# Summing modulation rows over partitions: on VectorE by 32x32 blocks, with one TensorE batch per phase

## The reference

```
def modulate(x, w, shift, scale):
    return rmsnorm(x, w) * (1 + scale) + shift

def modulation(cond, w_mod, b_mod):
    m = jax.nn.silu(cond) @ w_mod + b_mod
    return jnp.split(m, N_MOD, axis=-1)
...
        sh1, sc1, g1, sh2, sc2, g2, sh3, sc3, g3 = modulation(c[:, None, :], w_mod[l], b_mod[l])
        ch1, cs1, cg1, ch2, cs2, cg2, ch3, cs3, cg3 = modulation(c_ctx[None, None, :], w_mod[l], b_mod[l])
...
        x = x + 0.5 * g1 * swiglu(modulate(x, nw[0], sh1, sc1), ffn1_up[l], ffn1_down[l])
```

## Time and profile before

| | |
|---|---|
| median of three executions | 3129.01 us |
| profiled execution, whole | 3129.19 us |
| its span in the trace | 3127.4 us |
| mean granted TensorE clock | 0.99 |
| TensorE products busy | 3052.9 us, 98% |
| VectorE busy | 1511.2 us, 48% |
| ScalarE busy | 810.9 us, 26% |
| GpSimd busy | 213.0 us, 7% |
| read from HBM | 269.77 MB, mean 87 GB/s |

### The profile page before, as it was taken

The page is one execution under the profiler, slowest core; times in us unless marked ns, Lnnn a source line. Parts: engine busy times, 40 slices in busy tenths (PEclk is TensorE's granted clock), DMA queues, the critical chain, the costliest instruction groups (busy, mean ns, idle before and its releaser), DMA issues.

```text
span 3127.4 us, 43300 instructions
## 1 busy us (share of the span) xinstructions
PE 3052.9 (98%) x16692; PEld 2597.6 (83%) x16692; DVE 1511.2 (48%) x2649; ACT 810.9 (26%) x1094; POOL 213.0 (7%) x212
## 2 busy tenths in 40 slices
PE   7999999999999999999999999999999899999998
PEld 3888888888888888888888888888888778878886
DVE  2555565557533346656655652222236654443333
ACT  2221111233332232212112311121224333332223
POOL 1000000011600010000000100000010510100001
PEclk8999999999999999999999999999999999999999
DMA  6344343221112224344342332222112113333331
GB/s 207 95 127 115 109 129 112 76 69 48 28 41 63 72 61 131 103 128 121 113 127 79 95 104 61 61 60 67 57 46 68 48 51 97 98 87 94 94 93 63
DMA packets 455603, 273.42 MB, mean 87 GB/s; under 512 B 9754, under 2 KB 453828, under 8 KB 455492
## 3 DMA queue, kind: packets, MB, share of 16 engines
q1 hardware_dynamic: 453348, 267.90, 29.9%
q10 hardware_dynamic: 2144, 4.00, 0.4%
HBM read 269.77 MB, written 2.10 MB: 87 GB/s over the span
## 4 chain that ended last, share of the span: by engine, by line
PE 91%; DVE 5%; ACT 2%; issue 1%; DMA 0%; POOL 0%; ACTq 0%; DVEq 0%; POOLq 0%
PE ps L1221 53%; PE ps L1228 27%; PE ps L1371 2%; PE ps L1292 2%; PE ps L1252 1%; PE ps L1376 1%; PE ps L1331 1%; DVE hlo L1716 1%; DVE states L1033 1%; DVE htmp L1706 1%; PE ps L673 1%; PE ps L1270 1%; PE ps L642 1%; PE ps L653 1%; PE ps L557 0%
## 5 line engine op out<-in xcount | busy, mean ns | idle before, releaser
L1221 PE MATMUL ps<-hhi,whi 128*128 128x512 f32 x3136 | 901.0, 355 | 0.0
L1221 PE MATMUL ps<-hlo,whi 128*128 128x512 f32 x3136 | 887.1, 350 | 0.0
L1635 DVE TENSOR_TENSOR wlo<-wraw,whi 128x1024 fp32r<-128x1024 f32 x371 | 456.8, 1232 | 654.7 <-ACT whi L1465 651.0
L1465 ACT ACTIVATE whi<-wraw 128x1024 fp32r<-128x1024 f32 x371 | 391.5, 1056 | 1019.8 <-PE ps L1228 988.3
L1228 PE MATMUL ps<-hhi,wlo 128*128 128x512 f32 x3136 | 633.5, 351 | 0.0
L1221 PEld LDWEIGHTS ps<-hhi,whi 128*128 128x128 f32 x3136 | 503.2, 189 | 84.3 <-issue 3.1
L1221 PEld LDWEIGHTS ps<-hlo,whi 128*128 128x128 f32 x3136 | 502.4, 189 | 85.1 <-issue 0.5
L1228 PEld LDWEIGHTS ps<-hhi,wlo 128*128 128x128 f32 x3136 | 500.5, 188 | 84.7 <-issue 1.0
L1650 DVE SCALAR_TENSOR_TENSOR macc<-modraw,cond,macc 128x256 f32<-128x256 f32 x896 | 365.5, 479 | 0.0
L1221 PE MATMUL ps<-mhi,whi 128*128 128x512 f32 (+1 forms) x1184 | 335.8, 351 | 2.6 <-DVE mlo L1848 1.5
L1221 PE MATMUL ps<-mlo,whi 128*128 128x512 f32 (+1 forms) x1184 | 334.3, 349 | 0.0
(11 more groups left out here) (180 smaller groups left out, 2373.2 us busy)
## 6 DMA issues: line engine op xcount, KB each, us to landing
wraw<-in_ffn_up SPq DMA_DIRECT2D x176, 512.0 KB, 3.9
modraw<-in_w_mod SPq DMA_DIRECT2D x66, 1024.0 KB, 5.2
wraw<-in_ffn_down SPq DMA_DIRECT2D x64, 512.0 KB, 3.7
wraw<-in_w_in SPq DMA_DIRECT2D x64, 512.0 KB, 4.0
wraw<-in_ffn_down SPq DMA_DIRECT2D x32, 384.0 KB, 3.1
wraw<-in_w_out SPq DMA_DIRECT2D x16, 512.0 KB, 3.6
first_mod<-in_w_mod SPq DMA_DIRECT2D x6, 1024.0 KB, 12.0
wraw<-in_w_br_pool SPq DMA_DIRECT2D x16, 256.0 KB, 2.7
```

Of the source, the lines that this page charges most:

```text
L1221: nc.tensor.matmul(o, whi[:, slot, k, :], a[:, k * NT + t0:k * NT + t0 + n], start=(k == 0 and a is hi), stop=False)
L1465: nc.scalar.activation(whi[:, slot2], wraw[:, slot4], ACT.Copy).then_inc(hi_split, 1)
L1635: nc.vector.tensor_tensor(wlo[:, slot2], wraw[:, slot4], whi[:, slot2].bitcast(F32), ALU.subtract).then_inc(lo_split, 1)
```

## The change

It has three parts.

In the loop, VectorE does the sum over partitions nearly by itself. `mod_reduce` turns `macc` (128 x 512) in blocks of 32 x 32, so that what stood on 32 partitions stands in 32 neighbouring columns, and adds these. Four groups of 32 partitions are left, 16 columns for a job (`mred`). TensorE adds the four groups once per phase instead of once per job: `mod_sums` is four products with `fold`, a 128 x 32 matrix of four stacked identities. They run behind the first unit of the next phase, and `mod_finish` follows in VectorE's first pair of that phase, for all jobs of the phase before; gates made from them move behind it. The first pair of such a phase is taken out of the loop.

At the start, VectorE makes jobs 0 to 3 in two groups (`first_accumulate`), and one-column products sum them (`first_sums`); TensorE makes jobs 4 to 7 in the old way. The transfers go in the order 0, 1, 4, 5, 2, 3, 6, 7.

ScalarE takes the norm's root ahead of its first two weight splits, and the semaphore of the constants is cut in two, so that TensorE's first instruction waits for the identity and not for the mask.

```
+FIRST_ORDER = (0, 1, 4, 5, 2, 3, 6, 7)
...
+    fold = sb("fold", [P, BLK])
...
+    def jobs_pending(ph):
+        before = plan[plan.index(ph) - 1] if ph is not plan[0] else ph
+        return before if before["jobs"] and ph is not plan[0] else None
...
-            def mod_sums(job, buf):
-                pe.wait_ge(mod_step, DC * 2 * (job + 1 - START_JOBS))
-                for c in range(2):
-                    for h in range(2):
-                        mm = nc.tensor.matmul(bank(6, 2 * c + h, 1), macc[:, buf, c, h * P:(h + 1) * P],
-                                              ones[:, 0:1], start=True, stop=True)
+            def mod_sums(ph):
+                n0, n1 = jobs_of(ph)
+                pe.wait_ge(mod_reduced, n1 - START_JOBS)
+                at = plan.index(ph) % 2, n0 - ph["job"], n1 - ph["job"]
+                for q in range(P // BLK):
+                    mm = nc.tensor.matmul(bank(6, 0, 4 * (n1 - n0))[BLK * q:BLK * (q + 1)], fold[:],
+                                          mred[:, at[0], at[1]:at[2], q:JOB_COLS:P // BLK], start=True, stop=True)
                 mm.then_inc(mod_sum, 1)
...
-            pe.wait_ge(s_const, 32)
+            pe.wait_ge(s_ident, 16)
...
-            pe.wait_ge(cond_ready, 1)
-            both = cond[:].rearrange("p (c k) -> p k c", c=2)
-            for j in range(START_JOBS):
-                if j == START_JOBS // 2:
-                    norm_sum(BOTH, SQ_ADDED, DC)
-                    pe.wait_ge(rec_ready, 1)
...
+            first_products(VEC_JOBS)
+            first_products(VEC_JOBS + 1)
+            norm_sum(BOTH, SQ_ADDED, DC)
+            first_sums(0)
+            pe.wait_ge(rec_ready, 1)
+            for b in range(NBLK):
+                mm = nc.tensor.transpose(bank(6, b * P, P), tok[:, b:b + 1].to_broadcast([P, P]), ident[:])
+            mm.then_inc(bc_ready, 1)
+            first_products(VEC_JOBS + 2)
+            transpose_first_mod(0)
+            first_products(VEC_JOBS + 3)
+            first_sums(1)
+            transpose_first_mod(1)
...
-                            if jobs:
-                                mod_sums(j0 + 2 * i + h, (j0 + h) % 2)
+                                if first and isinstance(i, int) and i == 0 and jobs_pending(ph):
+                                    mod_sums(jobs_pending(ph))
...
+            act.wait_ge(set_up, 1)
+            root(0, BOTH)
             split_hi(0, 0, 0)
-            act.wait_ge(set_up, 1)
             split_hi(*second_unit(plan[0]))
-            root(0, BOTH)
...
+            def mod_reduce(ph, job, buf, i, h):
+                dve.wait_ge(mod_step, DC * 2 * (job + 1 - START_JOBS))
+                nc.vector.transpose(htmp[:, 0, 0:4 * P], macc[:, buf].rearrange("p c n -> p (c n)")).then_inc(mod_turned, 1)
+                dve.wait_ge(mod_turned, job + 1 - START_JOBS)
+                at = JOB_COLS * (8 * (plan.index(ph) % 2) + h)
+                nc.vector.tensor_reduce(mred[:].rearrange("p a j n -> p (a j n)")[:, ds(2 * JOB_COLS * i + at, JOB_COLS)],
+                                        htmp[:, 0, 0:4 * P].rearrange("p (j n) -> p j n", n=BLK),
+                                        mybir.AxisListType.X, ALU.add).then_inc(mod_reduced, 1)
...
+            def first_accumulate(i):
+                for j in (2 * i, 2 * i + 1):
+                    dve.wait_ge(first_loaded[j], 16)
+                columns = first_mod[:, 2 * i:2 * i + 2]
+                for k in range(DC):
+                    if i == 1 and k == DC // 2:
+                        reciprocals(0, BOTH)
+                    for c in range(2):
+                        acc = first_acc[:, 2 * i:2 * i + 2, c, :]
+                        scalar = cond[:, c * DC + k:c * DC + k + 1]
+                        if k == 0:
+                            ins = nc.vector.tensor_scalar(acc, columns[:, :, 0, :], scalar, None, ALU.mult)
+                        else:
+                            dve.wait_ge(first_step, 2 * DC * i + 2 * k - 1 + c)
+                            ins = nc.vector.scalar_tensor_tensor(out=acc, in0=columns[:, :, k, :], scalar=scalar, in1=acc,
+                                                                 op0=ALU.mult, op1=ALU.add)
+                        ins.then_inc(first_step, 1)
...
+                            if h == 0 and isinstance(i, int) and i == 0 and jobs_pending(ph):
+                                mod_finish(jobs_pending(ph))
+                                if needs_gates:
+                                    make_gates()
                             if jobs:
                                 mod_accumulate(job, (j0 + h) % 2, range(DC // 2, DC))
+                                mod_reduce(ph, job, (j0 + h) % 2, i, h)
```

More of the change, by code:

```diff
@@ L60 @@
 SQ_ADDED = DC - 2
-FIRST_BANKS = (4, 0, 1, 2)
+FIRST_BANKS = (4, 0)
+VEC_JOBS = 4
+BLK = 32
+JOB_COLS = 2 * 2 * P // BLK
+FIRST_ORDER = (0, 1, 4, 5, 2, 3, 6, 7)
 POOL_REC = GRID_H + GRID_W
@@ L248, in build @@
     mrow = lay("mrow", [P, 4 * P])
[L249 removed]
+    mod_row = lay("mod_row", [P, 2 * P * (START_JOBS - VEC_JOBS)])
+    lay.done()
+    lay = Layout()
+    lay.skip(111, "pad_first")
+    first_acc = lay("first_acc", [P, VEC_JOBS, 2, 2 * P])
     lay.done()
@@ L487, in tail_slots, with jobs_of @@
         return (whi, wlo, unit % 2) if s < 2 else (whi_more, wlo_more, s - 2)
+    def jobs_of(ph):
+        n0 = ph["job"] + (2 if ph is plan[0] else 0)
+        return n0, n0 + ph["jobs"]
     def jobs_before(ph):
@@ L520, in is_branch_ahead, with batches_before @@
         return ph["kind"] == "gates" and isinstance(i, int) and i == h == 0 and s == 2
+    def jobs_pending(ph):
+        before = plan[plan.index(ph) - 1] if ph is not plan[0] else ph
+        return before if before["jobs"] and ph is not plan[0] else None
+    def batches_before(ph):
+        return sum(1 for p in plan[:plan.index(ph)] if p["jobs"])
     def peeled(ph, a):
-        return (a == 0 and (follows_norm(ph) or ph["kind"] == "gates")) or (a == 1 and ph is plan[0])
+        return (a == 0 and (follows_norm(ph) or ph["kind"] == "gates" or jobs_pending(ph) is not None)) \
+            or (a == 1 and ph is plan[0])
     def proj_tensor(pe, l, u0, p0, unit_products, first_pair, inside):
@@ L1309, in _, with first_products @@
             pe.wait_ge(set_up, 1)
+            both = cond[:].rearrange("p (c k) -> p k c", c=2)
+            def first_products(j):
+                pe.wait_ge(cond_ready, 1)
+                pe.wait_ge(first_loaded[j], 16)
+                if j >= VEC_JOBS + 2:
+                    pe.wait_ge(xt_used, DC)
+                for k in range(DC):
+                    mm = nc.tensor.matmul(first_mod_ps(j), both[:, k, :], first_mod_columns(j)[:, k, :],
+                                          start=(k == 0), stop=(k == DC - 1))
+                mm.then_inc(mod_sum, START_JOBS // VEC_JOBS)
             def transpose_first_mod(i):
@@ L1641, in mod_accumulate @@
                     dve.wait_ge(mod_loaded[buf], 8 * job + (16 - 8 * buf - 8 * START_JOBS))
-                    at_least(dve, mod_sum, job - 1)
                 for k in ks:
@@ L1790, in _ @@
             dve.memset(eps[:], EPS).then_inc(set_up, 1)
+            dve.wait_ge(s_ident, 16)
+            steps.link(nc.vector.tensor_tensor(fold[:], ident[:, 0:BLK], ident[:, BLK:2 * BLK], ALU.add))
+            for q in (2, 3):
+                steps.link(nc.vector.tensor_tensor(fold[:], fold[:], ident[:, BLK * q:BLK * (q + 1)], ALU.add))
             dve.wait_ge(vec_t, 1)
@@ L1812, in _, with make_gates @@
                     continue
-                if (kind == "down" and ph["third"] == 0) or kind == "out":
+                def make_gates(kind=kind, l=l, ph=ph):
                     w = {"out": 5}.get(kind, 2 + 6 * ph["ffn"])
@@ L1820, in _ @@
                                                            1.0 if kind == "out" else 0.5, None, ALU.mult))
+                needs_gates = (kind == "down" and ph["third"] == 0) or kind == "out"
+                if needs_gates and not jobs_pending(ph):
+                    make_gates()
                 m0 = m_base(l, ph["ffn"], ph["third"])
@@ L1879, in body @@
                                                         ALU.subtract).then_inc(m_ready, 1)
-                            if jobs:
-                                mod_finish(job, (j0 >= MODJ) * 1)
                     repeat(dve, a, b, peeled(ph, a), body)
```

82 lines of the change are left out of this document (48 added, 34 removed).

## The result

The changed kernel takes 3034.88 us (median of four executions, 3032.96 to 3039.79) against 3128.41 us for the kernel before on the same chip: ratio 0.9703, 95% interval 0.969 to 0.9715. That is 93.5 us less; 76.2 were forecast. So the sign was right and the size was not, and the question of the experiments is where the other 17 us come from. The profiled execution took 3036.34 us, its span is 3034.6, its mean granted clock 0.99.

What follows compares the result with a forecast made beforehand. TensorE's stream was taken as the bound (91% of the chain). Loop -64.9 and start -11.3 sum to -76.2 us, from 3129.19 to 3053.0 us; range 3046 to 3065, or 3043 to 3072 with rivals 1 to 3.

Steps and rivals of the forecast that it cites:

- 8.48 us a unit: Feed-forward loop: a weight unit is 5.65 + 2.83 us of TensorE products; two units make the new job period, 16.96 us.
- Loop: Modulation jobs in the loop: -73.1 us for removed sums, +6.6 for batches, +1.6 for new waits, together -64.9 us.
- The batches: Four products with fold behind a phase's first unit: 0.6 us each, eleven cost 6.6 us (3.7 to 12.1).
- The new waits at the late pairs: First pairs behind a norm: TensorE waits 0.8 us for upper weights, twice, 1.6 us (0.5 to 4).
- VectorE's side: Loop jobs: transpose and reduction take 1.35 us a job (0.8 to 2.6), hidden in idle time before mtmp in ordinary pairs.
- The start: Up to the first real product: jobs 0 to 3 on VectorE bring it from 70.79 to 59.5 us, 11.3 us earlier.
- The lock: Start: VectorE's two-input steps and GpSimd's sums take turns at the SBUF inputs; first group ends at 36.4 us.
- rival 1: Start: the lock does not bite; first product at 55.0 us, total 3048.5 us; chance 0.12.
- 2 (the start gains less): Start: last job and sums also run at the low clock; first product at 63.7 us, total 3057; chance 0.13.
- 3 (dear batches): Loop: 2 us a batch from draining, or clock falls at the two new waits; +21 us, total 3074; chance 0.08.
- 4 (VectorE the bound): Loop pairs: at 8 us a job for transpose and reduction the period is 19.3 us, total 3200; chance 0.02.
- 5 (nothing gained): Loop: the removed 0.89 us return as another wait, above all for weights; time the same; chance 0.03.

Runs made afterwards that it cites:

- the gap kernel: Kernel before plus only an unused tensor of 128 bytes per partition where the change puts fold: 3112.89 us, ratio 0.9944.
- the change without its shift: Changed kernel with fold moved to the free end of memory, so activations lie where the kernel before has them: 3052.53 us, ratio 0.9758.
- the 32-byte gap: Kernel before with 32 unused bytes per partition ahead of the activations, rounded weights unmoved: 3108.23 us, ratio 0.9933.

## Why the prediction was right in the sign and wrong in the size

**The step that failed is the sum's silent one: that the products left in the stream keep their pace, "8.48 us a unit".** The prediction took TensorE's stream as fixed but for the instructions added and removed, and had no term for where the new constant is allocated. That term is 15.4 us by the gap kernel and 17.6 by the change without its shift, with units of 5.50 in place of 5.60 us and in some stretches of 8.37 in place of 8.48. The range did not hold the time for the same reason: all its bounds were bounds of instructions. The change without its shift took 3052.5 us, where the forecast was 3053.0: the terms that the prediction did have add up rightly, by small misses of both signs. Why the distance between the operands changes the pace stays open.

**Loop: forecast -64.9; measured -65.3** where all units have the old paces, and -66.3 beside the shift. The regular jobs: the sums and their 0.89 us each are gone. The batches cost less than the 0.6 us each of the forecast: in the kernel without the shift, where the units around them all take 8.48 us, 0.38 to 0.42, and 4.4 us for the eleven in place of 6.6, close to the lower bound, the 0.34 us of four small transposes. A batch's weight load of 32 columns takes 108 ns and its product 204 (median of 88 each). The new waits at the late pairs: forecast 0.8 us twice, found 0.8 and 0.4, together 1.2 in place of 1.6.

One term the prediction did not have. In each of the two networks with jobs, at the change to its last "down" phase (near 572 and 1645 us), TensorE needs the mlo of the pair just finished at once. Before, a job's sums stood there and filled the time; now it waits 0.7 us, twice, and its waits for mlo at that line are 2.9 us in place of 1.5. So -73.1 + 4.4 + 1.2 + 1.4 = -66.1, against -65.3.

**VectorE's side: forecast 1.35 us a job, measured 0.71 + 0.69 = 1.40**, hidden in all ordinary pairs; of 3.83 us idle 2.94 - 1.35 = 1.6 should have been left and 2.37 were; where the other 0.8 come from was not looked into. The Trainium skill ("VectorE: DVE Perf Modes", "The three transpose paths" for the transpose, "Rules for kernel authors" for the reduction as the slowest VectorE operation) gave an estimate of 2.5 us. Here the reduction of 128x512 takes 686 ns, less than the transpose, and less than the 748 ns of a two-input operation of that size. The measurement decides against that estimate.

**The start: forecast -11.3; measured -10.5 alone, and -11.8 on top of the loop,** the latter with a part that is pace. The milestones: first group's end 36.4 forecast, 36.0 found; reciprocals done at 41.7, found 40.9; third TensorE job done 49.0, found 46.9, for it took 4.48 us and not 5.79; last job 52.9, found 50.8; first product 59.5, found 57.45. So 2 us more than forecast at the first product, and 2 us lost again before the end, most of them in the first mixer, for which the prediction had no term. That these two cancel is luck. The lock is there, in turns as forecast: of the first group's fourteen steps three take 2.29 us each, beside GpSimd's sums of 1.81 to 2.07, and the eleven behind the last sum 0.74. It is stronger than the forecast had it, since the two one-input operations were slowed too (1.20 and 2.04 us in place of 0.47); it costs less at the first product than rival 1 said: without it that comes at 56.98, not at 55.0. Rival 1 left out the column sums of the first group, which end at 39.88 us and stand ahead of TensorE's broadcast; its broadcast could begin at 37.2.

**The rivals.** 2 (the start gains less), 3 (dear batches), 4 (VectorE the bound) and 5 (nothing gained) did not happen: 2.37 us of idle time and 0.38 to 0.42 us a batch exclude 4 and 3. Rival 1's total of 3048.5 is nearer to the time than the forecast, but not for its reason. Rival 2's reason did not show: the last job took 3.55 us, as at the full clock. What came was a case that no rival had.

## What to carry to other kernels

In a kernel that TensorE bounds at nearly full clock, a new tensor in the on-chip memory is a change of its own, even one of 128 bytes. Compare the pace of identical products in a stretch that the change does not reach, and in more than one, for here it changed inside a run; if it differs, run the kernel before with an unused tensor of that size in the same place, and the change with its tensor elsewhere, before any microsecond is credited to the idea. And where the stream of products is tight, try the order of the allocations: here 64 bytes gave the kernel before 34 us, about half of what the reworked loop gave.

## What the runs showed of the hardware

- TensorE's products of one shape at one clock differ by up to 3% in pace with the distance between the moving operand and the weights in a partition: 5.60, 5.58, 5.50 or 5.44 us for 24 products of 512 columns. Moving both by 128 bytes changes nothing (3128.8 us); distances of 20224 and 20480 bytes give the same paces. Why is open.
- A unit of 512 + 256 columns and one of 512 alone answer to different distances (96 bytes more: 8.32 and 5.60 us; 128 bytes more: mostly 8.48, and 5.50).
- At some distances the units of 512 + 256 columns have two paces in one execution, 8.48 us and 8.32 or 8.37, and change over where the stream is interrupted (the 32-byte gap at 1211 us, the changed kernel at 272 and 406). At the old distance all of them take 8.48. What decides is open. At 64 bytes more the time also spreads more from one execution to the next: 3086 to 3105 us, and 3091 to 3105 with the weights moved by 192, against 3127 to 3131 before.
- A transpose of 128x512 float32 in 32x32 blocks takes 712 ns on VectorE, and a reduction from 512 to 16 columns 686 ns.
- GpSimd's sums of two 768-column inputs slow VectorE's one-input operations as well: 3.16 us for two that take 0.89 otherwise. That is more than the prediction's turns between operations of two inputs. A step of two inputs takes 2.29 us in such a turn and 0.74 alone.
